# An attention block that gives its output accumulator a second PSUM bank, and its small products three banks in place of four

## The reference

```
def gqa_attention(q, k, v):
    scale = q.shape[-1] ** -0.5

    def attend(qb):
        s = jnp.einsum('bkgqd,bksd->bkgqs', qb, k).astype(jnp.float32) * scale
        p = jax.nn.softmax(s, axis=-1).astype(v.dtype)
        return jnp.einsum('bkgqs,bksd->bkgqd', p, v)

def diff_attention(q, k, v, lam):
    ...
        a = jax.nn.softmax(s1, axis=-1) - lam32 * jax.nn.softmax(s2, axis=-1)
        return jnp.einsum('bhqs,bhsd->bhqd', a.astype(v.dtype), v)
```

## Time and profile before

| | |
|---|---|
| median of 3 runs | 2312.03 us (2311.45 to 2313.1) |
| profiled execution | 2315.04 us |
| its span, first to last instruction | 2313.2 us |
| PE / DVE / POOL / ACT busy | 91% / 61% / 41% / 37% |
| one attention block | some 480 us, twice |

### The profile page before, as it was taken

The page is one execution under the profiler, slowest core; times in us unless marked ns, Lnnn a source line. Parts: engine busy times, 40 slices in busy tenths (PEclk is TensorE's granted clock), DMA queues, the critical chain, the costliest instruction groups (busy, mean ns, idle before and its releaser), DMA issues. The chain is left out here.

```text
span 2313.2 us, 28623 instructions
## 1 busy us (share of the span) xinstructions
PE 2099.9 (91%) x10525; PEld 1474.2 (64%) x10525; DVE 1409.4 (61%) x2322; ACT 854.5 (37%) x1760; POOL 958.6 (41%) x512
## 2 busy tenths in 40 slices
PE   3799999898999999979837999998989999999798
PEld 1578898665555555537716788986655555555386
DVE  1668300296788788876516673003967887888774
ACT  1432221333555555442124322214335555554421
POOL 0211111243888888840002111112438888887400
PEclk9999999798999999999969999998989999999899
DMA  7342221201111110024363322212011111100243
GB/s 276 105 123 87 73 64 58 49 2 43 20 20 26 27 20 19 14 88 131 108 263 109 117 91 69 64 60 48 2 43 20 20 26 27 20 19 14 101 120 107
DMA packets 188757, 155.74 MB, mean 67 GB/s; under 512 B 125181, under 2 KB 150209, under 8 KB 186561
## 3 DMA queue, kind: packets, MB, share of 16 engines
q1 hardware_dynamic: 185424, 153.35, 22.0%
q10 hardware_dynamic: 3184, 0.47, 0.1%
HBM read 115.37 MB, written 38.42 MB: 66 GB/s over the span
## 5 line engine op out<-in xcount | busy, mean ns | idle before, releaser
L1159 POOL TENSOR_TENSOR prob_sums<-prob_sums,probs 128x1024 f32<-128x1024 f32 x246 | 586.8, 2385 | 72.7 <-ACT probs L1324 44.5
L1324 ACT ACTIVATE probs<-scores 128x512 f32<-128x512 f32 x672 | 360.8, 603 | 374.5 <-PE scores L1219 159.0
L501 POOL TENSOR_TENSOR w_lo<-w_stage,w_hi 128x512 fp32r<-128x512 f32 (+1 forms) x112 | 134.5, 1232 | 824.2 <-ACT w_hi L436 824.2
L1390 DVE TENSOR_REDUCE neg_max_parts<-work 128x1 f32<-128x512 f32 (+1 forms) x640 | 396.1, 684 | 68.2 <-PE work L1197 62.8
L403 PE MATMUL z_acc<-w_hi,h_hi 128*128 128x512 f32 (+1 forms) x640 | 237.7, 371 | 11.7 <-DVE h_lo L520 8.9
L403 PE MATMUL z_acc<-w_lo,h_hi 128*128 128x512 f32 (+1 forms) x640 | 234.9, 367 | 0.0
L403 PE MATMUL z_acc<-w_hi,h_lo 128*128 128x512 f32 (+1 forms) x640 | 234.7, 367 | 0.0
L825 DVE MEMSET k_stackB<- 128x24 f32 (+1 forms) x4 | 0.9, 218 | 346.6 <-PEq L287 346.6
L403 PE MATMUL z_acc<-h_hi,w_lo 128*128 128x512 f32 (+1 forms) x528 | 187.0, 354 | 0.0
L403 PE MATMUL z_acc<-h_hi,w_hi 128*128 128x512 f32 (+1 forms) x528 | 186.9, 354 | 0.0
L403 PE MATMUL z_acc<-h_lo,w_hi 128*128 128x512 f32 (+1 forms) x528 | 186.7, 354 | 0.0
(11 more groups left out here) (244 smaller groups left out, 3781.6 us busy)
## 6 DMA issues: line engine op xcount, KB each, us to landing
w_stage<-in_w_in SPq DMA_DIRECT2D x96, 256.0 KB, 3.0
mod_w<-in_w_mod SPq DMA_DIRECT2D x16, 1024.0 KB, 14.2
z_scratch<-z_out SPq DMA_DIRECT2D x60, 256.0 KB, 2.0
cv<-u_scratch SPq DMA_DIRECT2D x20, 512.0 KB, 6.3
mod_w<-in_w_mod SPq DMA_DIRECT2D x16, 512.0 KB, 21.1
u_scratch<-z_out SPq DMA_DIRECT2D x32, 256.0 KB, 2.0
out_y_sample<-y_tiles SPq DMA_DIRECT2D x16, 512.0 KB, 5.1
q_rawA<-z_scratch SPq DMA_DIRECT2D x16, 320.0 KB, 4.0
```

Of the source, the lines that this page charges most:

```text
L501: pool.tensor_tensor(w_lo[:, n % RING, 0:cols], stage[:, n % STAGES, 0:cols], w_hi[:, n % RING, 0:cols].bitcast(F32), ALU.subtract).then_i ...
L1159: ins = pool.tensor_tensor(a, a, pr[:, n % NPB, :], ALU.add)
L1324: act.activation(pr[:, n % NPB, c * NB:(c + 1) * NB], sc[m % SCORE_BANKS][:, :], ACT.Exp, scale=SCALE[u]).then_inc(s["a_exp"], 1)
L1390: dve.tensor_reduce(dst, src, AX_X, ALU.max, negate=True).then_inc(s["a_wkdve"], 1)
```

## The change

`att_out` becomes two banks, used by even and odd units in turn: `weigh(p, 0)` no longer waits for `output(p - 1)` but for `output(p - 2)`. The bank comes from the work banks, of which there are three now, so that use x waits for the read of use x - 3. There are eight PSUM banks, three of them for scores.

```
-SCORE_BANKS, WORK_BANKS = 3, 4
+SCORE_BANKS, WORK_BANKS, OUT_BANKS = 3, 3, 2
...
-        ob = ctx.enter_context(nc.psum_tensor("att_out", [P, NB], F32))
+        ob = [ctx.enter_context(nc.psum_tensor(f"att_out{i}", [P, NB], F32)) for i in range(OUT_BANKS)]
...
-                    pe.wait_ge(s["a_out"], p + 1)
+                    pe.wait_ge(s["a_out"], max(p + 2 - OUT_BANKS, 1))
...
-                        mm = pe.matmul(ob[rows, :], v[u][:, j, :], probs[:, q], start=(j == 0), stop=(j == KT_S - 1))
+                        mm = pe.matmul(ob[p % OUT_BANKS][rows, :], v[u][:, j, :], probs[:, q], start=(j == 0), stop=(j == KT_S - 1))
...
-                weighted(p, ob, rs, 0, NB).then_inc(s["a_out"], 1)
+                weighted(p, ob[p % OUT_BANKS], rs, 0, NB).then_inc(s["a_out"], 1)
```

## The result

The changed kernel takes 2364.97 us (median of 4 runs, 2363.07 to 2366.8), the kernel before 2312.57 in the same comparison (4 runs): a ratio of 1.0224, 95% interval 1.0209 to 1.0239. It is 52 us slower; the forecast was 40 us slower, 2352, with a range to 2366. The profiled execution took 2365.95 us, its span is 2364.2.

A forecast was written before the change was run, and what follows sets the result against it. PE was taken as the bound, any new wait on it paid in full. Per block 16.5 (odd units) + 1.9 (unit 7) + 1.8 (sums) - 0.3 = 19.9 us, twice 39.8: from 2312.0 to 2352 us, range 2338 to 2366.

The forecast's parts named there:

- What is removed: PE's wait for VectorE's read of `att_out` before weighing in unit 15: a gain of 0.3 us per block, 0.6 us.
- The prompt's product: In odd units PE starts it later, waiting for VectorE's read of prep 3: 1.57 us (four units) or 1.50 (two).
- group 1: First prep group behind the prompt's product in odd units: claimed to cost nothing beyond the prompt's wait.
- Groups 2 and 3: Odd units: each group's last prep waits for VectorE's fourth read instead of the third, 0.60 us per group, not caught up.
- Unit 7: The unit that prepares new keys: later key preps and slower groups, about 1.9 us.
- Even units: Groups and prompts cost nothing; only the sums, waiting for ScalarE's read of prep 27, start 0.18 us later.
- The sum: All forecast losses less the gain: 19.9 us per block, twice 39.8.
- The clock: Rival: after the 1.5 us pause in odd units the granted clock falls, 14 x 3.5 = 49 us on top, 2401; 7%.
- the full version: Clock rival at full size: half speed for one group per odd unit, 49 us on top, 2401 us; 7%.
- few single clock falls: Allowance for isolated drops of the granted clock, included with some half-loss cases when the range was set at 2338 to 2366.
- Half the loss: Rival: the groups' 0.60 us are caught up and only the prompts' waits stay, 22 us, 2334; 10%.
- The marks I named: Signs forecast in the profile: odd units 29.5 us, L1241 idle 1.5 us twelve times, L1197 waits some 8 us, PE busy 2100.

## Why the prediction was right, point by point

- **What is removed: 0.6 us.** Right in kind, a little small. The end of the block gave 0.52 us per block rather than 0.3 (with one output bank and three work banks it gave nothing), and nothing elsewhere shows a gain; the two runs with four work banks show no other gain.
- **The prompt's product.** 1.57 us later were forecast, 1.58 measured in unit 5, with an idle of 1.4 to 1.5 us in all twelve places, and group 1 adds nothing to it with three banks. Shown by the order in time, and its parts by the runs that take the wait away or add it alone.
- **Groups 2 and 3, 0.60 each.** Group 2 takes 0.61 us more, group 3 0.59. At the end of group 3 PE is 2.78 us late, where I had 2.77. The unit in all grew by 2.62: 0.16 is caught up at its end, where the sums used to wait for POOL's additions. I had not counted that wait.
- **Unit 7: 1.9 forecast and 0.18 for its sums, 2.1 measured. Even units: some 0.2 against 0.18.** The total of the even units is right, its parts are not. In unit 4 the sums start 3.21 us behind the last weighing (703.17 to 706.38) against 3.13 before (693.01 to 696.14), so the sums' wait is 0.08 us. Another 0.08 is lost before that: the last weighing itself starts 26.37 us behind the reciprocal that begins the unit (676.80) against 26.29 (666.72), where I had put the groups of even units at nothing. That the two together come near 0.18 is luck.
- **The sum** without the clock would be 49.7 - 12.6 = 37.1 us against 39.8.
- **The clock.** This is the step that was mis-sized: "at 1.00 through the block with the pauses there are" was true of the kernel before and was read as a promise for the one after. The falls came as the rival said, behind the wait in odd units, but at 1.6 us each in 8 of the 14 odd units (none of them a unit 7), in place of 3.5 us in each of the 14: 12.6 us, not 49. With the forecast at 80% and the full version at 7%, the small version, which is what happened, had no more room than the "few single clock falls" for which the range was widened, 4 us above 2362. That the median, 2365, lies inside the range, whose end is 2366, is in part luck: it took the 2.7 us by which the rest came out smaller, and one of the four runs (2366.8) lies outside. The row that I held against it (scores 0.49 us apart at 1.00) had no pause of 1.5 us in it.
- **Half the loss** did not happen. Of its mechanism (a PE that comes later finds its inputs ready) only the 0.16 us at the sums of an odd unit shows. A recovery of another kind is in the run with four banks and the wait alone: there half of the wait comes back, most of it in the group behind it. So "any new wait on PE is paid in full" is not true of that kernel.
- **The marks I named.** Odd units 29.5: 29.35, if the clock holds. L1241 with 1.5 us, twelve times: yes. VectorE's idle 1.1 us: yes. Two were wrong: PE's busy time did not stay at 2100 us, and the waits of L1197 do not appear in PE's list; they are idle time of the weight loads (32.3 us to 48.6 in this block), and the mean record of L1197 grew.

The row of L1197 with A's keys on the page of the changed kernel (before, the same 416 took 126.0 us, 398 ns each):

```profile
L1197 PE MATMUL work<-kTA,qTA 128*128 128x512 f32 (+1 forms) x416 | 145.7, 432 | 6.0 <-DVE qTA L1376 1.8
```

## What to carry to other kernels

A rotation of N buffers is not judged by the list of waits. Before you take one away, ask of each use how long after the read of the use N - 1 before it the engine starts: that is what it will wait for. A start right behind the read of the use N before it (0.06 us here) says that the rotation is already full, whatever the idle column says. Here a bank moved from such a rotation to one with 0.2 us of slack, and the kernel lost. When a change brings a pause such as this one of 1.5 us to a TensorE that was dense, give a small cost of the clock, in a part of the places, a chance of its own, between none and everywhere. And ask what stands behind a new wait: a later wait that it hides (here POOL's, 0.16 us) gives part of it back, and work moved out of the way of one kind of unit can cost the other kind more.

## What was not expected of the hardware

- One product of a prep (`L1198`, fp32r) set between two tiles of weighing (fp32) costs 0.37 us more than the same products in two runs of their kind. The first weight load of a prep behind a weighing has 0.81 us of weight-load idle ahead of it, in an even unit as in an odd one. The two kinds differ in type and in the width of their weights (128 and 64 columns), and no run tells which of these it is.
- The granted clock fell behind a pause of 1.5 us in 8 of 12 places in the change, 8 of 12 with three work banks and one output bank, 2 of 12 with the pause alone, 2 of 12 with the pause and the seventh prep moved, and 0 of 12 in each of the four kernels with three work banks and no such pause, and in the kernel before. It also fell in 3 of 12 with two score banks, one output bank and no such pause. Outside the twelve places, a unit 7 has a fall in six of the kernels. The counts are of one execution each. The pause matters, since the four kernels with three work banks and without it show none; what follows it may matter too; what decides in which places the clock falls stays open. The Trainium skill ("TensorE: Matmul & The Clock Gate", A second HAM failure mode: psum-queue depth-cycling) describes small pauses at banks that make the clock swing. Here the clock fell behind the pause of 1.5 us at a bank, at 1.6 us each time; shorter pauses at banks, up to 0.6 us in the run with the prompt's product behind the weighing, brought none in the twelve places.
